# Last stage of a transformer layer with experts: three row sums to VectorE and GpSimd, four final products to GpSimd and ScalarE, and three row buffers zeroed one stage earlier

## The reference

```python
xp = xp + g1 * y
xp = xp + g2 * hier_moe(modulate(xp, norm_ffn[l], sh2, sc2), *moe_w)
y_prompt = rmsnorm(xp, norm_final)
```

## Time and profile before

| what | value |
|---|---|
| median of 3 runs | 1263.89 us (1262.38 to 1266.19) |
| profiled execution, its own time | 1264.53 us |
| its span, first to last instruction | 1262.7 us |
| mean granted TensorE clock, share of 2.4 GHz | 0.946 |
| TensorE matmuls busy | 1114.2 us (88%) |
| VectorE busy | 495.5 us (39%) |
| ScalarE busy | 354.9 us (28%) |
| GpSimd busy | 362.7 us (29%) |
| HBM traffic over the span | 195 GB/s |

### The profile page before, as it was taken

One profiled execution on the slowest core, in us unless ns is written; L12 is line 12 of the kernel. 1 busy time (PEld: TensorE's weight loads), 2 busy tenths in 40 slices (PEclk: granted clock), 3 DMA queues, 4 the chain that ended last, 5 costly groups with the idle time before them and its releaser, 6 DMA issues. The chain is left out here.

```text
span 1262.7 us, 20112 instructions
## 1 busy us (share of the span) xinstructions
PE 1114.2 (88%) x7198; PEld 777.1 (62%) x7198; DVE 495.5 (39%) x1303; ACT 354.9 (28%) x1124; POOL 362.7 (29%) x306
## 2 busy tenths in 40 slices
PE   3678999999999999999997799981999999989956
PEld 1435988888888888888886588861333333333322
DVE  2432144444444445354456157665121121121227
ACT  4432033433433333334345222210111111011102
POOL 3030253534544221305004135544222222121001
PEclk9778999999999999999999799995899999999978
DMA  9863040424232221303039422133999999999775
GB/s 367 331 252 120 17 120 30 125 68 128 68 107 68 82 83 51 80 2 113 1 93 326 157 84 68 67 118 127 399 368 400 383 413 404 402 367 424 292 277 179
DMA packets 86793, 238.62 MB, mean 189 GB/s; under 512 B 10448, under 2 KB 58008, under 8 KB 75936
## 3 DMA queue, kind: packets, MB, share of 16 engines
q1 hardware_dynamic: 68368, 132.00, 29.9%
q10 hardware_dynamic: 7344, 78.91, 15.4%
q0 software_dynamic: 10976, 26.32, 5.6%
HBM read 208.19 MB, written 38.45 MB: 195 GB/s over the span
## 5 line engine op out<-in xcount | busy, mean ns | idle before, releaser
L1806 PE MATMUL moe_gu_ps<-a_gu,moe_xT_sb 128*64 x416 | 185.4, 599 | 6.7 <-DMA b_gu<-in_w_gu 4.7
L853 PE MATMUL att_piece_ps<-hT_hi,w_hi 128*128 128x384 f32 (+1 forms) x528 | 186.0, 352 | 2.3 <-PEq L186 0.9
L1809 PE MATMUL moe_gu_ps<-b_gu,moe_xT_sb 128*64 128x512 f32 x416 | 185.4, 599 | 0.0
L853 PE MATMUL att_piece_ps<-hT_hi,w_lo 128*128 128x384 f32 (+1 forms) x528 | 174.6, 331 | 0.0
L853 PE MATMUL att_piece_ps<-hT_lo,w_hi 128*128 128x384 f32 (+1 forms) x528 | 174.0, 330 | 0.0
L1049 DVE COPY att_pT_sb<-att_pT_ps 128x512 f32<-128x512 f32 (+2 forms) x192 | 94.5, 520 | 134.6 <-PE att_pT_ps L921 131.6
L1806 PEld LDWEIGHTS moe_gu_ps<-a_gu,moe_xT_sb 128*64 128x64 f32 x416 | 57.1, 138 | 127.4 <-issue 127.3
L1115 ACT ACTIVATE att_probs_sb<-att_probs_sb,att_nmax_sb 128x640 f32<-128x640 f32 (+5 forms) x144 | 101.2, 703 | 43.5 <-DVE att_nmax_sb L1035 42.8
L1133 ACT ACTIVATE keep_rows_all_sb<-att_o_ps,att_rden_sb 128x64 f32<-128x64 f32 x144 | 37.3, 309 | 247.0 <-PE att_o_ps L942 247.0
L853 PEld LDWEIGHTS att_piece_ps<-hT_hi,w_hi 128*128 128x128 f32 x528 | 100.4, 190 | 9.8 <-issue 4.8
L1035 DVE CUSTOM_DVE_ANT_0 att_probs_sb<-att_s_ps,att_bias_sb 128x640 f32<-128x640 f32 (+5 forms) x144 | 95.2, 662 | 27.3 <-PE att_s_ps L909 15.0
(11 more groups left out here) (301 smaller groups left out, 1986.6 us busy)
## 6 DMA issues: line engine op xcount, KB each, us to landing
b_gu<-in_w_gu ACTq DMA_DIRECT2D x25, 2048.0 KB
b_dn<-in_w_dn ACTq DMA_DIRECT2D x25, 1024.0 KB
a_gu<-in_w_gu SPq DMA_DIRECT2D x10, 2048.0 KB, 12.3
keep_rows_all_sb<-in_w_ada SPq DMA_DIRECT2D x8, 2048.0 KB, 11.6
att_w_raw_sb<-in_w_qkv SPq DMA_DIRECT2D x21, 512.0 KB, 3.7
a_dn<-in_w_dn SPq DMA_DIRECT2D x10, 1024.0 KB, 20.0
in_w_ada_sb<-in_w_ada SPq DMA_DIRECT2D x4, 2048.0 KB, 10.9
w_out_parts<-keep_rows_all_sb SPq DMA_DIRECT2D x16, 512.0 KB, 5.0
```

Of the source, the lines that this page charges most:

```text
L853: ins = pe.matmul(bank[:, 0:hi - lo], w[:, kind, kc, :], x[:, kc, lo:hi], start=(m == 0), stop=(m == 3 * NC - 1))
L1806: pe.matmul(gu_ps[p % 2][LANE[0], :], xT[:, c, LANE[0]], a_gu[:, bass.ds(slot, 1), c, :].rearrange("p a n -> p (a n)"), start=(c == 0), st ...
L1809: ins = pe.matmul(gu_ps[p % 2][LANE[1], :], xT[:, c, LANE[1]], b_gu[p % 3][:, c, :], start=(c == 0), stop=(c == NC - 1))
```

## The change

In the last stage:
- The sum of tile 0 is made by VectorE from SBUF (`DVE_SUM`), the sums of tiles 1 and 8 by GpSimd, in place in `ya` (`POOL_SUM`), those of tiles 2 to 7 by TensorE as before (`PE_SUM`).
- For tiles 1, 3, 5 and 7 (`POOL_NORM`) VectorE's normalise is gone. GpSimd multiplies `ya` by `norm` into `yb` once the residual is done, and ScalarE scales that by the reciprocal root with a copy, behind the square of the next tile. SP stores these tiles from `yb`.
- GpSimd's order is: sum of tile 1; then for each tile its product, if it has one, and its two small operations; the sum of tile 8 stands ahead of the product of tile 3.

Ahead of the expert loop, the memsets of the three buffers `x` move from `experts`, where they stood between the first three listings and the first gather, to the end of `mix_out`: behind GpSimd's loop over tiles and a wait for the last tile of `h2`, and ahead of the scatters of tiles 7 and 8.

```diff
+        pool.wait_ge(h2_ready, TILES)
+        for j in range(3):
+            pool.memset(k["x"][j][:, :], 0.0).then_inc(x_zeroed, 1)
         for t in GROUPS[-1]:
             scatter(t)
+        pool.wait_ge(x_zeroed, 3)
         pool.wait_ge(listed, 32 * TILES)
...
+    DVE_SUM, POOL_SUM, PE_SUM = (0,), (1, NT), range(2, NT)
+    POOL_NORM = (1, 3, 5, 7)
...
-            sp.wait_ge(out_ready, t + 1)
-            sp.dma_start(dst, ya[0:r, t, :]).then_inc(stored, 16)
+            if t in POOL_NORM:
+                sp.wait_ge(out_act, POOL_NORM.index(t) + 1)
+            else:
+                sp.wait_ge(out_ready, t + 1 - sum(u < t for u in POOL_NORM))
+            sp.dma_start(dst, (yb if t in POOL_NORM else ya)[0:r, t, :]).then_inc(stored, 16)
...
         for p in range(3):
             listing(p)
-        for j in range(3):
-            pool.memset(x[j][:, :], 0.0).then_inc(x_zeroed, 1)
-        pool.wait_ge(x_zeroed, 3)
         for p in range(3):
             gather(p)
...
+        def rows_sum(t):
+            r = rows_of(t)
+            pool.wait_ge(back[t], 32)
+            pool.tensor_tensor(ya[0:r, t, :], ya[0:r, t, :], yb[0:r, t, :], ALU.add).then_inc(pool_summed, 1)
+
+        rows_sum(POOL_SUM[0])
         for t in range(TILES):
             r = rows_of(t)
+            if t == 3:
+                rows_sum(POOL_SUM[1])
+            if t in POOL_NORM:
+                pool.wait_ge(x_done, t + 1)
+                pool.wait_ge(norm_ld, 16)
+                pool.tensor_tensor(yb[0:r, t, :], ya[0:r, t, :], norm[0:r, :], ALU.mult).then_inc(normed, 1)
             pool.wait_ge(sq_done, t + 1)
...
-        for t in range(TILES):
+        for t in PE_SUM:
             r = rows_of(t)
             pe.wait_ge(back[t], 32)
-            if t >= 3:
+            if t >= PE_SUM[0] + 3:
                 pe.wait_ge(gated, t - 2)
...
+            if t - 1 in POOL_NORM:
+                act.wait_ge(normed, POOL_NORM.index(t - 1) + 1)
+                act.wait_ge(rstd_done, t)
+                act.activation(yb[:, t - 1, :], yb[:, t - 1, :], ACT.Copy, scale=rstd[:, t - 1:t]).then_inc(out_act, 1)
...
-            dve.wait_ge(summed, t + 1)
-            dve.tensor_tensor(out, sum_ps[t % 3][0:r, :], g2[0:r, cond_of(t), :], ALU.mult).then_inc(gated, 1)
+            if t in PE_SUM:
+                dve.wait_ge(summed, t - PE_SUM[0] + 1)
+                total = sum_ps[t % 3][0:r, :]
+            elif t in POOL_SUM:
+                dve.wait_ge(pool_summed, POOL_SUM.index(t) + 1)
+                total = out
+            else:
+                dve.wait_ge(back[t], 32)
+                dve.tensor_tensor(out, out, yb[0:r, t, :], ALU.add).then_inc(dve_summed, 1)
+                dve.wait_ge(dve_summed, DVE_SUM.index(t) + 1)
+                total = out
+            dve.tensor_tensor(out, total, g2[0:r, cond_of(t), :], ALU.mult).then_inc(gated, 1)
             dve.wait_ge(gated, t + 1)
             dve.tensor_tensor(out, out, rows_all[0:r, t, :], ALU.add).then_inc(x_done, 1)
...
         for t in range(NT):
             residual(t + 1)
-            normalise(t)
+            if t not in POOL_NORM:
+                normalise(t)
         normalise(NT)
```

More of the change, by code:

```diff
@@ L1222, in mix_out @@
     lg_ps, pos_ps = s.ps("lg", [P, 2, 256]), s.ps("pos", [P, 512])
-    ld, zeroed, half_set, x_ld = s.sem("ld"), s.sem("zeroed"), s.sem("half_set"), s.sem("x_ld")
+    ld, zeroed, half_set, x_ld, x_zeroed = (s.sem(n) for n in ("ld", "zeroed", "half_set", "x_ld", "x_zeroed"))
     oT_ready, oT_upper, oT_out = s.sem("oT_ready"), s.sem("oT_upper"), s.sem("oT_out")
@@ L1643, in experts @@
     slot_ld = [first_a] + [s.sem(f"slot_ld{n}") for n in range(1, SLOTS)]
-    x_zeroed = s.sem("x_zeroed")
+    pool_summed, dve_summed, normed, out_act = (s.sem(n) for n in ("pool_summed", "dve_summed", "normed", "out_act"))
     own_dve, cols_done, table_ready, table_set = s.sem("own_dve"), s.sem("cols_done"), s.sem("table_ready"), s.sem("table_set")
```

## The result

The changed kernel takes 1269.12 us (median; 1266.06 to 1272.9) against 1262.89 for the one before on the same chip (1259.5 to 1266.19). The ratio is 1.0046, with a 95% interval of 1.0029 to 1.0064, so it is 0.46% slower; the medians differ by 6.2 us. The forecast was 1267.3, 3.4 us slower than 1263.89, with a range of 1260.0 to 1269.8. The profiled execution of the changed kernel took 1272.9 us, its span is 1271.1, its mean granted TensorE clock 0.932.

A forecast was written before the change was run, and what follows sets the result against it. TensorE was taken to bound the middle of the expert loop, VectorE the last stage. Profiled 1264.53 - 0.7 (memsets) + 4.1 (last stage) = 1267.9, less 0.64 to the median: 1267.3 us against 1263.89, range 1260.0 to 1269.8.

The forecast's parts named there:

- Memsets, -0.7 us: Expert loop's start: moving the memsets starts the first gather 0.9 us earlier, of which 0.7 us comes off the path.
- rival 4: Expert loop's start: the memsets were the whole wait, 3.2 us off instead of 0.7; chance 0.15 within each other case.
- One way into SBUF, by turns: Last stage: VectorE instructions with both inputs in SBUF and GpSimd instructions exclude each other, the waiter getting a whole turn.
- Any GpSimd instruction: Last stage: what VectorE's instructions with two SBUF inputs were taken to exclude; the multiply from PSUM was taken to exclude none.
- Rival 2: Last stage: the engines don't hinder each other at this size, so it ends 2.6 us early, 1260.6 us; chance 0.20.
- Rival 3: Last stage: holds are real but short (products of 1.9 us, or free small operations), +1 to +2 us; chance 0.20.
- Tiles 0 to 2: Last stage's start: early sums on VectorE and GpSimd bring tile 2's multiply to 1228.2 instead of 1229.90, 12.1 us in.
- the term's bounds: TensorE's first sum in the last stage: low clock for 5.5 to 7.5 us, moving the result about 0.8 us either way.
- Tiles 2 to 8: Last stage from tile 2's multiply to the last normalise: 32.0 us, holds and late roots ending it 4.1 us late.
- both adds are held 1.04 us, the first by GpSimd's sum of tile 8: Last stage, tiles 4 and 5: GpSimd's tile 8 sum delays VectorE's add 4, product 3 delays add 5, 1.04 us each.
- rival 1: Last stage: GpSimd takes each turn first, normalises 4 and 6 wait 2.24 us each, stage +5.4 us, 1268.6; chance 0.15.
- my own case: Last stage: the forecast itself, stage +3 to +5 us with a range of 1266 to 1269.5 us; chance 0.45.

The follow-up runs named there:

- experiment 1: The kernel before with only the three memsets moved to their new place, last stage untouched: 1262.04 us, ratio 0.9988 to the kernel before.
- experiment 5: The changed kernel with each of GpSimd's four products replaced by three memsets of the same tile, which only write: one run, 1264.48 us.
- experiment 9: The changed kernel with SP loading tile 8's rows behind tile 2's instead of last: 1268.78 us, ratio 1.0044 to the kernel before.
- experiment 6: The changed kernel with tile 8's sum back on TensorE, GpSimd keeping tile 1's sum and four products: 1264.84 us, ratio 1.001 to the kernel before.
- experiment 4: The changed kernel with all nine sums back on TensorE, keeping the products on GpSimd and ScalarE: 1270.84 us, ratio 1.005 to the kernel before.
- experiment 2: The changed kernel with the memsets back where they were, so only the last stage is changed: 1268.64 us, ratio 1.0038 to the kernel before.
- experiment 12: Changed kernel with VectorE summing tiles 0 and 1, TensorE the rest, VectorE all normalises, plus 22 filler products ahead of TensorE's sums: 1275.05 us, ratio 1.0095.

## Why the prediction was right in direction and short by 3 us

**Memsets, -0.7 us.** The steps held: the first gather then waits for its list, it starts 1.2 us earlier counted from the first listing (forecast 0.9), VectorE's long instruction is short, the new place costs nothing (10.40 us of its gap are left). The gain was lost one step later, in the gather's own transfer (6.23 us instead of 5.20). From listing to transpose the changed kernel measures -0.18 us and experiment 1 +0.03. That puts rival 4, the whole 3.2 us, out; experiment 1's interval alone would not.

**One way into SBUF, by turns.** Right for GpSimd instructions that read SBUF, and shown by experiment 5. "Any GpSimd instruction" was too wide: memsets don't hold the normalises. Rival 2 is out: three holds of 5.89 us in all. Rival 3 is out too: products take 2.34 us, not 1.9, and the small operations do wait: one column took 1.05 to 1.11 us instead of 0.19, and 1.41 to 1.51 instead of 0.55.

**Tiles 0 to 2, forecast 12.1 us to the multiply of tile 2.** It was 10.94. TensorE started 5.69 us behind VectorE's first sum (forecast 5.4), but its sum took 5.25 us instead of 6.6: it ran at the low clock for about 3.1 us, until shortly before the row at 1227.14, where the kernel before did until about 1222, 5.8 us into its own. That is below the 5.5 to 7.5 us that I had as the term's bounds, and the change didn't cause it: in experiment 1 the unchanged stage got the high clock after 3.2 us as well. I had taken one profile's clock for the stage's. The head start was 2.8 us against that profile and 1.5 against experiment 1, not 1.7.

**Tiles 2 to 8, forecast 32.0 us.** It was 35.37, and here the step failed that reads "both adds are held 1.04 us, the first by GpSimd's sum of tile 8". Add 4, due at 1236.56 and held 1.04 us, means that this sum ends at 1237.6, so that it has to run from 1235.2, 19.1 us behind the stage's first sum. I never asked whether its rows are there by then. Even at 412 GB/s the 7.9 MB behind tile 0's rows take 19.1 us, all of the time that the forecast had. The sum started at 22.0, behind 6.39 us of idle. An estimate for the difference: at 194 instead of 407 GB/s the half tile's 0.52 MB take 1.4 us more; the first stores share the DMA engines by then, too, and what they cost wasn't measured. In GpSimd's queue product 3 and the small operations of tiles 3 and 4 stood behind it, so root 4 came at 1247.6: 18.5 us behind the multiply of tile 2, where the forecast had 15.8. Normalise 4 then waited 4.06 us instead of 1.8. So 2.8 of the 3.4 us that the forecast was short stand there when normalise 4 starts; from there to the last normalise it is 16.8 us against 16.2. Experiment 9 takes the lateness away, and the part behind the cut is 32.41, 0.4 from the forecast; experiment 6 takes the sum away, and it is 30.29. Of the 9.20 us lost there, about 5.1 are tile 8's sum (35.37 less 30.29), 3.0 of these its lateness (35.37 less 32.41), and the other 4.1 are the products. The parts don't simply add: alone, the sums cost 4.93 and the products 5.96.

**Which instructions are held.** I had adds 4, 5 and 6 at 1.04 us each and multiply 8 at 2.3. Only add 5 was held, 1.74; instead normalises 4 and 6 were, 2.08 each, and multiply 8 ran in 1.21. That is rival 1's mechanism, to which I gave 0.15: product 5 starts at 1247.58 and normalise 4 at 1247.65. It accounts for 0.6 us of the miss at most, though, since both holds lie behind the start of normalise 4; and experiment 9 has the same two holds and is near the forecast.

**Sum.** Last stage +6.4 instead of +4.1, memsets about -0.2 instead of -0.7: 6.2 instead of 3.4 us. Two misses partly cancel in this: the part ahead of the cut came out 1.2 us shorter than forecast, by the clock, and the part behind it 3.4 us longer. There is luck in the range as well: the kernel before ran 1.0 us faster this time, and the ratio applied to 1263.89 gives 1269.7, at the edge of the range. A stage 6.4 us longer lies outside the +3 to +5 of my own case, and what was measured, clearly slower, had a chance of 0.35 against 0.50 for no change. The tail behind the last normalise was the same (6.67 and 6.63 us), as forecast.

## What to carry to other kernels

Work moved to GpSimd can cost VectorE a whole turn wherever GpSimd reads SBUF while VectorE takes two inputs from there, and more than it saves once VectorE waits for GpSimd's small results: moving four normalises of 1.2 us cost 4.1 to 6.0 us. Before an instruction is put into an in-order queue, look when its data land, and what stands behind it; one early wait of 6.4 us for the last tile's rows cost about 3 us, most of it in front of a normalise that has nothing to do with that tile. And cut a stage at the instruction where its head start ends: the gain (1.5 to 2.8 us) and the loss (9.2) were two effects, and only the first was worth keeping. Take the clock's rise from more than one profile before it becomes a term of a sum.

## What the runs showed of the hardware that was not expected

- GpSimd's next instruction starts about 0.07 us ahead of VectorE's that waits for the one before it (1247.58 and 1247.65; 1256.45 and 1256.52; 1236.64 and 1236.71 in experiment 4): with a reading instruction queued behind the release, GpSimd gets the turn, in all eleven such meetings in five profiles (the changed kernel and experiments 2, 4, 6 and 9), and the normalise takes 3.35 to 3.36 us.
- Memsets of GpSimd don't hold VectorE's instructions with two SBUF inputs (1.28 us in experiment 5), though in the kernel before an instruction with one took 3.24 us beside memsets, and 0.44 without them.
- While loads into 64 partitions are among those on the way, all together run at 194 GB/s with the DMA engines full; loads into 128 partitions run at 407 (experiment 9).
- The same stage with the same instructions had the low clock for 5.8 us in the kernel before and for 3.2 in experiment 1.
- TensorE starts nothing for 13 to 15 us behind the expert loop's last product, even what waits for nothing, while VectorE starts 11.3 us behind that product when its rows are there (experiment 12). What holds it isn't shown. The Trainium skill ("Runtime: NRT & Kernel Launch", section "Instruction fetch mechanics") says that a taken branch out of the loaded pages forces a fetch before execution goes on, which would fit; no run here shows it.
